# Expert gates written by indirect adds to DRAM tables, instead of one-hot matmuls

## The reference

```
q = (h @ wq).reshape(B, T, 8, 2, 128)                      # 8 heads, two halves
s = einsum('bthpd,pnd->bthpn', q, subkeys)                 # 128 scores for each half
s_top, i_top = top_k(s, 16)
cand = s_top[..., 0, :, None] + s_top[..., 1, None, :]     # 16 x 16 sums
best, pos = top_k(cand.reshape(..., 256), 16)
experts = 128 * i_top[0][pos // 16] + i_top[1][pos % 16]   # one of 16384
gates = softmax(best)
a = einsum('td,tkd->tk', h, u[experts])
y = einsum('tk,tkd->td', gates * gelu(a), v[experts])
```

## Time and profile before

| | us |
|---|---|
| median of 3 runs | 3919.49 (3919.15 to 3920.51) |
| the profiled execution, its span | 3916.3 |
| PE busy | 3864.7 (99% of the span) |
| DVE busy | 2781.5 (71%) |
| ACT busy | 1523.5 (39%) |
| POOL busy | 1321.6 (34%) |

### The profile page before, as it was taken

The page is one execution under the profiler, slowest core; times in us unless marked ns, Lnnn a source line. Parts: engine busy times, 40 slices in busy tenths (PEclk is TensorE's granted clock), DMA queues, the critical chain, the costliest instruction groups (busy, mean ns, idle before and its releaser), DMA issues.

```text
span 3916.3 us, 48823 instructions
## 1 busy us (share of the span) xinstructions
PE 3864.7 (99%) x18074; PEld 3129.0 (80%) x18074; DVE 2781.5 (71%) x4585; ACT 1523.5 (39%) x2251; POOL 1321.6 (34%) x758
## 2 busy tenths in 40 slices
PE   7999999999999999999999999999999999999999
PEld 5767878888888888888877678788888888888887
DVE  5736557987777758888776363589787776588886
ACT  4537433343333333333344373433433333433332
POOL 2432333440000017777334223334300000387772
PEclk9999999999999999999999999999999999999999
DMA  7635333667776579999746432237677765899995
GB/s 286 226 124 170 113 128 108 226 228 263 266 260 222 204 260 391 364 359 358 269 162 222 134 130 81 82 118 242 232 260 262 258 241 180 305 376 372 353 354 198
DMA packets 411869, 918.97 MB, mean 235 GB/s; under 512 B 38416, under 2 KB 176528, under 8 KB 410032
## 3 DMA queue, kind: packets, MB, share of 16 engines
q1 hardware_dynamic: 327664, 664.77, 49.2%
q0 software_dynamic: 45056, 134.38, 9.2%
q10 hardware_dynamic: 38976, 117.66, 7.8%
HBM read 794.00 MB, written 256.90 MB: 268 GB/s over the span
## 4 chain that ended last, share of the span: by engine, by line
PE 83%; issue 7%; DVE 4%; POOL 4%; ACT 1%; DMA 1%; ACTq 0%; POOLq 0%; SPq 0%; DVEq 0%
PE ps L1057 14%; PE ps L1058 14%; PE ps L1059 14%; PE ps L1075 10%; PE ps L1077 10%; PE ps L1076 10%; POOL w_lo L1007 4%; PE ps L1432 2%; PE ps L1333 1%; PE ps L1337 1%; PE ps L1335 1%; PE ps L1300 1%; PE ps L1314 1%; PE ps L1290 1%; PE ps L1251 1%
## 5 line engine op out<-in xcount | busy, mean ns | idle before, releaser
L598 ACT ACTIVATE w_hi<-raw 128x1024 fp32r<-128x1024 f32 x504 | 534.3, 1060 | 1595.1 <-PE ps L1059 1316.1
L1057 PE MATMUL ps<-h_hi,w_hi 128*128 128x512 f32 x2768 | 1086.5, 393 | 5.1 <-POOL w_lo L1007 3.5
L1058 PE MATMUL ps<-h_hi,w_lo 128*128 128x512 f32 x2768 | 1080.1, 390 | 0.0
L1059 PE MATMUL ps<-h_lo,w_hi 128*128 128x512 f32 x2768 | 1079.5, 390 | 0.0
L1007 POOL TENSOR_TENSOR w_lo<-raw,w_hi 128x1024 fp32r<-128x1024 f32 x242 | 614.4, 2539 | 1101.1 <-ACT w_hi L598 1101.1
L1012 POOL DMA_INDIRECT acts<-expert_act,e_act x256 | 381.6, 1491 | 1244.9 <-DMA expert_act<-gel 1167.5
L1057 PEld LDWEIGHTS ps<-h_hi,w_hi 128*128 128x128 f32 x2768 | 519.2, 188 | 122.4 <-issue 8.9
L1059 PEld LDWEIGHTS ps<-h_lo,w_hi 128*128 128x128 f32 x2768 | 518.5, 187 | 112.2
L1058 PEld LDWEIGHTS ps<-h_hi,w_lo 128*128 128x128 f32 x2768 | 518.8, 187 | 100.9
L1867 DVE TENSOR_TENSOR w_lo<-raw,w_hi 128x1024 fp32r<-128x1024 f32 x192 | 235.1, 1224 | 277.1 <-ACT w_hi L598 277.1
L1020 POOL DMA_INDIRECT down<-expert_down,e_row x256 | 325.3, 1271 | 210.6 <-DVE y L2004 87.8
(11 more groups left out here) (288 smaller groups left out, 6070.2 us busy)
## 6 DMA issues: line engine op xcount, KB each, us to landing
raw<-in_stream_dram SPq DMA_DIRECT2D x648, 512.0 KB, 3.5
expert_down<-in_stream_dram SPq DMA_DIRECT2D x256, 512.0 KB, 5.2
expert_act<-gel ACTq DMA_DIRECT2D x256, 256.0 KB, 2.1
raw_more<-in_stream_dram SPq DMA_DIRECT2D x128, 512.0 KB
expert_gate<-gatebuf ACTq DMA_DIRECT2D x12, 4096.0 KB, 12.9
a_in<-expert_act SPq DMA_DIRECT2D x128, 384.0 KB
g_in<-expert_gate SPq DMA_DIRECT2D x128, 384.0 KB
ada_first<-in_stream_dram SPq DMA_DIRECT2D x8, 1024.0 KB, 17.9
```

Of the source, the lines that this page charges most:

```text
L598: return act.activation(o, i, ACT.Copy)
L1057: pe.matmul(o, w_hi[:, s, w], mov_hi[:, c, :], start=c == 0, stop=False)
L1058: pe.matmul(o, w_lo[:, s, w], mov_hi[:, c, :], start=False, stop=False)
L1059: mm = pe.matmul(o, w_hi[:, s, w], mov_lo[:, c, :], start=False, stop=c == KC - 1)
```

## The change

Gates no longer go through PE. For tiles 1 to 3, DVE computes for each pick the address in the gate table (`gate_i`) and the gate (`gate_v`), and POOL adds the gates into a zeroed table in DRAM, one indirect DMA for 128 tokens and one pick: 3 tiles x 128 picks = 384 of them in a layer. Two picks of one token can be the same expert, in different heads, so POOL waits before each 16 adds until the earlier ones of that tile have landed. There is a table for each layer, cleared by 12 DMAs of 2 MB from a block of zeros, among the mixer's loads. The picks are now made for two heads of all four tiles at a time (`choose`, `weigh`), so that adds can begin after a quarter of the search. POOL makes lower halves only up to unit 15; from 16 on DVE makes them all, one between any two steps of the search. The one-hot matmuls, the transposes and the stores of `gatebuf` are gone.

```diff
-    gate_d = nc.dram_tensor("expert_gate", (DSEQ // GT, P, NK, GT), F32, kind="Internal").ap()
+    gate_d = [nc.dram_tensor(f"expert_gate{l}", (NK * P * DSEQ, 1), F32, kind="Internal").ap() for l in range(DEPTH)]
+            def clear_gates(l, n):
+                rows = gate_d[l].rearrange("(n p r f) o -> n p r (f o)", n=CLEARS, p=P, f=512)
+                sp.dma_start(rows[n], zero_d.unsqueeze(1).to_broadcast([P, NK * P * DSEQ // (CLEARS * P * 512), 512])
+                             ).then_inc(gate_cleared, 16)
...
                 load_split(l, U_U + 124, 0)
-                for half in range(2):
-                    sp.wait_ge(gate_stored[half], 16 + (l + 1) * DT * 16)
+                for tt in range(DT):
+                    sp.wait_ge(gate_added[tt], (l + 1) * PICKS * 16)
...
+            def add_gate(l, n):
+                g, tt, k = n // (DT * 32), n // 32 % DT, n % 32
+                if tt == 0 and k == 0:
+                    pool.wait_ge(picked_ready, l * 4 + g + 1)
+                if k % TOPK == 0 and g * 2 + k // TOPK:
+                    pool.wait_ge(gate_added[tt], 16 * (l * PICKS + g * 32 + k))
+                h, c = 2 * g + k // TOPK, k % TOPK
+                pool.indirect_dma_start(out=gate_d[l],
+                                        out_offset=bass.IndirectOffsetOnAxis(ap=gate_i[:, tt, h, c:c + 1], axis=0),
+                                        in_=gate_v[:, tt, h, c:c + 1], in_offset=None, compute_op=ALU.add
+                                        ).then_inc(gate_added[tt], 16)
...
-                with pool.Fori(0, HOT0 // RAW) as i:
+                with pool.Fori(0, LOW0 // RAW) as i:
...
-                pool.wait_ge(index_ready, l + 1)
+                pool.wait_ge(gate_cleared, (l + 1) * CLEARS * 16)
+                for n in range(DT * PICKS):
+                    add_gate(l, n)
...
+                for g in range(4):
+                    pace = lower_next if g else lambda: None
+                    experts_of(2 * g, pace)
+                    if g:
+                        weigh(g - 1)
+                    experts_of(2 * g + 1, pace)
+                    choose(g, pace)
+                weigh(3)
+                while lowered < 124:
                     lower_next()
```

More of the change, by code:

```diff
@@ L163, in row_unit_of, with clears_by @@
     return ROW0 + k * (NK - 1 - ROW0) // PICKS
-def groups_before(e):
-    return e * 32 * DT // HOT_UNITS
+def clears_by(l, p):
+    first, last = PLACE[l]["w", U_V] - START[l], PLACE[l]["w", U_MIXB] - START[l]
+    return CLEARS * min(max(p - first + 1, 0), last - first) // (last - first)
 def pairs_lowered_at(n):
@@ L475, in load_listed @@
                         copy_down(l, n)
+                    for n in range(clears_by(l, p - 1) if p else 0, clears_by(l, p)):
+                        if l == 0 and n == 0:
+                            sp.wait_ge(zeros_stored, 16)
+                        clear_gates(l, n)
             sp.dma_start(silu_first[:], c_in).then_inc(c_loaded, 16)
@@ L957, in store_gates @@
[L957 to L971, removed]
@@ L973, in _ @@
-                for e0 in range(0, HOT_UNITS + 4, 4):
-                    experts(0, 4, HOT0 + e0, gates_after(e0))
+                with act.Fori(0, LOW0 // 4) as i:
+                    experts(i, 4, 0)
+                for e0 in range(LOW0, EXP_UNITS, 4):
+                    experts(0, 4, e0, gate_exp(e0))
+                with act.Fori(EXP_UNITS // 4, 31) as i:
+                    experts(i, 4, 0)
                 def pair_hi(j):
@@ L1409, in _ @@
                 experts(0, 4, 0, lambda b: score(15) if b == 0 else None)
-                with pe.Fori(1, PICK0 // 4) as i:
+                with pe.Fori(1, NK // 4) as i:
                     experts(i, 4, 0)
[L1412 to L1434, removed]
-                                mm.then_inc(hot_used, 1)
-                        return extra
-                    for k in range(units // 4):
-                        experts(i, units, HOT0 + 4 * k, gates(k))
-                for k in range((NK - HOT0 - HOT_UNITS) // 4):
-                    experts(0, 4, HOT0 + HOT_UNITS + 4 * k)
                 def sum_group(g, s, opens=False, closes=False):
@@ L1815, in top16 @@
                     settle(ins)
+                    between()
                 def sub_keys(n):
@@ new lines, in choose @@
+                        step(ins)
+                        step(dve.tensor_reduce(picked[:, side, :], match[:], AX_X, ALU.add))
+                    between()
+                    ids = e_id[:].rearrange("p t k -> p (t k)")
+                    step(dve.scalar_tensor_tensor(out=ids, in0=picked[:, 0, :], scalar=float(NK), in1=picked[:, 1, :],
+                                                  op0=ALU.mult, op1=ALU.add))
+                    dve.scalar_tensor_tensor(out=gate_i[:, :, hs, :].rearrange("p t h k -> p t (h k)"), in0=e_id[:, 1:TT, :],
+                                             scalar=float(DSEQ), in1=shift[:], op0=ALU.mult, op1=ALU.add)
@@ new lines, in _ @@
+                for tt in range(DT):
+                    ins = dve.tensor_scalar(shift[:, tt, :], const[:, C_TOKEN:C_TOKEN + 1].to_broadcast([P, 32]), float(tt * P),
+                                            None, ALU.add)
+                step(ins)
+                for g in range(4):
[5 more added lines that the diff above has]
+                    choose(g, pace)
```

243 lines of the change are left out of this document (74 added, 169 removed).

## The result

The changed kernel takes **4295.4 us** (median of 4 runs, 4290.4 to 4302.5) against 3919.3 before: the ratio is 1.096, with a 95% interval of 1.094 to 1.098. The forecast was 3869 with a range up to 4060. It is wrong in sign, and the time lies outside the range. The span of the profiled execution is 4295.1 us, that of before 3916.3: 378.8 more.

A forecast was written before the change was run, and what follows sets the result against it. PE, busy 99% of the span, was taken as the bound. Gates -52.6, handover +6.6, clears +3 and late adds +18 gave -25 a layer, -50 in all: 3869 us from 3919.3, range 3830 to 4060.

The forecast's parts named there:

- The gates' 52.6 us a layer: PE's expert stage: time over 5.44 us a unit in the three later stretches, saved when gates leave PE.
- The handover: DVE's search steps between lower halves: those too long make PE wait, 6.6 us a layer.
- the wait at unit 20: First quarter's weigh and the lower half end about 8.7 us after unit 18, against 5.44: PE waits 3.3.
- The clears: Clears of 2 MB among the mixer's loads, 5.6 us of queue each: cost 3 us a layer, between 0 and 12.
- The adds: POOL's 384 adds a layer, priced by its gather, end at 1381 against a deadline of 1363: 18 us late.
- The twelve waits: POOL's waits for fresh landings, at the 16th add of each tile: 3 us each, 12 a layer.
- DVE's two-input operations: A POOL operation waits for the rest of them: 0.13 us an add in the light part, 0.28 in the search.
- the 0.28 of the search: Mean delay in us of an add by DVE's operations during the search, giving 1.53 us an add.
- From the last add to unit 125: SP issues eight pair loads (7.9), load (3.5), split, lower half and handoffs (3.6) before PE's start: 15 us.
- Rival 2: An add costs POOL more than a gather: a quarter more gives 4060, half more 4230; chance 0.28.
- a quarter more: Rival 2's POOL time of 1.20 us an add: 96 us a layer, 4060; upper end of the range.
- Rival 1: Adds end before the deadline, at 1.37 us each instead of 1.42: 43 us a layer gained, 3833; chance 0.17.

The follow-up runs named there:

- e1: Changed kernel with the 384 indirect DMAs of a layer writing the gate instead of adding it, double picks not summed: 3868.1 us.
- e9: Changed kernel with plain writes instead of adds and the twelve clears of a layer at places off the next layer's modulation units: 3835.8 us.
- e5: Changed kernel with double picks summed ahead on DVE, plain writes, clears moved and the first Exp after unit 17 instead of 18: 4607.0 us.
- e6: Changed kernel with plain writes, double picks not summed, clears moved and the first Exp after unit 17 instead of 18: 4628.4 us.

## Why the prediction was wrong, point by point

**The gates' 52.6 us a layer** did leave PE. Units 52 to 124 take 391.6 us in e1, 72 x 5.44.

**The handover**, 6.6 us a layer, was too small. The wait at unit 20 was forecast at 3.3 and is 3.33. What was missed is what it does to PE's clock. Units 16 to 24 take 6.4 us more than 8 x 5.44, and the granted clock behind the wait, in the changed kernel, is half:

```profile
805.00:815.00 10.00, 10.00 (x46) 8.29 (x45) 1.24 (x2) 4.68 (x6) 0.00 (x0) 1.00 0.71 248
820.43:825.00 4.57, 4.57 (x11) 3.60 (x12) 4.42 (x16) 0.00 (x0) 3.66 (x4) 0.50 0.91 260
825.00:830.00 5.00, 5.00 (x21) 4.04 (x20) 1.15 (x6) 0.95 (x1) 4.39 (x3) 0.87 0.86 235
```

The half clock lasts until about 826.3. So a wait of 3.3 us cost 6.4 us in layer 1, and 5.2 in layer 2, where the half clock lasted 3.3 us. Units 24 to 52 add 4.3 (forecast 3.3): 10.7 in all in layer 1.

**The clears** were taken at 3 us a layer with a bound of 12; they cost 16.4 and 17.6. The step that failed is "at the rate that the DMA engines reach when full, 375 GB/s, that is 5.6 us". A clear took 12.6 us to land, 166 GB/s of writing. I had priced a copy inside DRAM by loads to SBUF. The nearer row stood in the same list, `expert_down` with 0.5 MB in 5.2 us: four of those would be 21 us.

**The adds** are the term that decided, and the step that failed is "The nearest row is POOL's gather: 0.94 us". Start, 799 forecast and 817 measured: the clears are 16 of the 18. Length, 582 us forecast and 776 measured (816.8 to 1592.8). Of the difference the adding is +230 (384 x 0.60). DVE's operations delayed an add by 0.075 us in the mean (1.623 less 1.548) and not by 0.168, which is -36. The twelve waits were 3.2 us each and not 3, +3. Sum: 197, against 194 found. That DVE's two-input operations hold up POOL was right in kind and more than twice too large: 74 of the 768 adds take over 1.65 us, and each of these started under a DVE `tensor_tensor`, while none of the 12 that started under the `tensor_reduce` of the picks was longer. By the terms named there, the 0.28 of the search should also have been 0.31, which is 3 us a layer.

**From the last add to unit 125**: 15 us forecast, 15.8 measured (1592.8 to 1608.6).

**Rival 2** had the mechanism as far as POOL's instruction goes, the place (SP's wait ahead of the pairs) and the slope. At 0.60 us more an add, its rule of 384 us a layer for each us gives 3869 + 2 x 230 = 4330, near the 4295 found. It was given 0.28, and the range was cut at a quarter more although half more was named. The argument held against it, that 4 KB and 4 bytes cost a gather the same, speaks of bytes. What differs in an add is the number of packets, 138 against 28, and of that the trace of before said nothing. That POOL's time goes with this number is not shown: the packets are five times as many, the time is 1.6 times as long. With a term that no row shows and a sign that turns at 0.065 us in 0.95, the bound should have stood at the far end. The forecast's own range was also added up short: its terms give 3839 to 3923, not 3838 to 3911.

**Rival 1** is what the change would be worth with plain writes and well-placed clears: 3833 forecast, 3835.8 in e9. That it is so close is in part luck: it has the clears at 3 us a layer, where e9 pays under 1, and the handover at 6.6, where e9's units 16 to 52 of layer 1 take 7.6 more than 36 x 5.44, and its writes still end late enough for a wait of 1.9 us at unit 125 of layer 1.

## What to carry to other kernels

When work moves to an idle engine as hundreds of small instructions, the price of one decides everything: work out at what price the sign turns, and if the trace has no row of that very form, measure one before building on it. Here a plain write cost POOL what a gather had (0.96 against 0.94 us), and an add did not (1.55). If the adding form is dear, make the sums on an engine with time to spare and write plainly: here that turned 9.6% slower into 1.9% faster. Put bulk clears where no other stream runs ahead of its use, and price them by a copy of their own kind.

## What the runs showed of the hardware

- An indirect DMA of 128 elements of 4 bytes occupies POOL for 1.55 us when it adds to its target and for 0.96 us when it writes, with 0.30 us to the next in both. Between 1000 and 1100 us adding took 22.6% of the DMA engines' time, at some 52 adds, and writing 1.6%, at some 79 writes.
- A clear of 2 MB from a small zero table in DRAM lands in 12.6 us. Twelve of them cost 16 to 18 us beside the mixer's first units (e1) and under 1 us at other places (e9).
- PE came back at half its clock (0.50 granted, the 1.2 GHz level) after a wait of only 3.3 us, for 5.9 us in layer 1 and 3.3 in layer 2. After the wait of 210 us it was 0.50 over the first 5.4 us and 0.93 over the next 6.0: the wait 60 times as long cost hardly more of the clock.
- An add that starts while DVE is in a `tensor_tensor` with two SBUF operands takes longer, up to 3.25 us; under the `tensor_reduce` of the picks it takes 1.55 as without.
- In two of seven kernels with unbroken plain indirect writes from POOL, at a step of 1.27 us, the other engines stalled for hundreds of us beside idle DMA engines (e5, e6). In the one kernel with a pause of 0.54 us on POOL after each fourth write there was no stall. The cause is open.
